# 23 modulation units summed on VectorE beside the feed-forwards, instead of matmuls on TensorE

## The reference, cut to what matters

```python
c_act = silu(c)                                          # one vector of 1024
for i in range(2):
    mod = (c_act @ mod_w[i] + mod_b[i])                  # mod_w[i]: 1024 x 9216
    shift, scale, gate = mod.reshape(1, 3, 3, 1024)[...] # one of each for each of three sublayers
    h = rms_norm(x, g[i,0]) * (1 + scale[0]) + shift[0]
    x = x + 0.5 * gate[0] * ffn(h, i, 0)                 # (silu(h @ w_gate) * (h @ w_up)) @ w_down
    h = rms_norm(x, g[i,1]) * (1 + scale[1]) + shift[1]
    x = x + gate[1] * mixer(h)                           # attention: "fox" for i=0, "dilated" for i=1
    h = rms_norm(x, g[i,2]) * (1 + scale[2]) + shift[2]
    x = x + 0.5 * gate[2] * ffn(h, i, 1)
# then the second block: two layers without modulation
```

## Time and profile before

| | |
|---|---|
| runs of before | 2365.1, 2369.22, 2369.62 us; median 2369.22 |
| profiled execution, its own time | 2364.49 us |
| its span | 2363.2 us |
| TensorE busy (matmuls) | 2260.6 us, 96% |
| VectorE busy | 1327.0 us, 56% |
| ScalarE busy | 1155.3 us, 49% |
| mean DMA rate | 186 GB/s, 439.75 MB |
| mean granted TensorE clock | 0.991 |

### The profile page before, as it was taken

One profiled execution on the slowest core, in us unless ns is written; L12 is line 12 of the kernel. 1 busy time (PEld: TensorE's weight loads), 2 busy tenths in 40 slices (PEclk: granted clock), 3 DMA queues, 4 the chain that ended last, 5 costly groups with the idle time before them and its releaser, 6 DMA issues.

```text
span 2363.2 us, 38278 instructions
## 1 busy us (share of the span) xinstructions
PE 2260.6 (96%) x16752; PEld 2060.3 (87%) x16752; DVE 1327.0 (56%) x1763; ACT 1155.3 (49%) x1348; POOL 57.2 (2%) x72
## 2 busy tenths in 40 slices
PE   6999998999999999899899999999999999999998
PEld 3999866999999987677699997899999988989998
DVE  2543565544455466657555445556786555667873
ACT  3443565543444354544554335654555456436553
POOL 2000000000000000000000011000000020000000
PEclk9999999999999999999999999999999999999999
DMA  8767562666575756345165555433655363445550
GB/s 311 236 229 289 196 250 68 218 223 231 187 252 196 266 192 247 128 150 205 56 214 183 192 196 175 161 125 125 211 182 191 126 233 132 154 143 179 179 196 19
DMA packets 273590, 439.75 MB, mean 186 GB/s; under 512 B 10656, under 2 KB 147152, under 8 KB 273296
## 3 DMA queue, kind: packets, MB, share of 16 engines
q1 hardware_dynamic: 270880, 429.07, 52.6%
q0 software_dynamic: 2256, 7.12, 0.9%
q10 hardware_dynamic: 288, 1.11, 0.1%
HBM read 436.22 MB, written 1.05 MB: 185 GB/s over the span
## 4 chain that ended last, share of the span: by engine, by line
PE 89%; ACT 5%; DVE 3%; DMA 1%; issue 1%; SPq 0%; POOL 0%; ACTq 0%; POOLq 0%; DVEq 0%
PE ps L1265 86%; ACT whi L1487 1%; DVE wlo L1674 1%; PE ps L1418 1%; ACT PT L1487 1%; PE ps L1365 1%; PE ps L1453 1%; DMA raw<-in_mod_w 1%; ACT xhi L1487 1%; PE ps L1428 1%; ACT L1487 1%; ACT S L1487 0%; DMA raw<-in_fox_w_in 0%; SPq L1254 0%; ACT x L1487 0%
## 5 line engine op out<-in xcount | busy, mean ns | idle before, releaser
L1674 DVE TENSOR_TENSOR wlo<-raw,whi 128x2048 fp32r<-128x2048 f32 x339 | 769.0, 2275 | 584.8 <-ACT whi L1487 584.6
L1487 ACT ACTIVATE whi<-raw 128x2048 fp32r<-128x2048 f32 x339 | 640.7, 1895 | 422.4 <-PE ps L1265 387.1
L1265 PE MATMUL ps<-xhi,whi 128*128 128x256 f32 x2888 | 733.5, 286 | 14.8 <-ACT xhi L1487 11.4
L1265 PE MATMUL ps<-xhi,wlo 128*128 128x256 f32 x2888 | 727.9, 284 | 0.0
L1265 PEld LDWEIGHTS ps<-xhi,whi 128*128 128x128 f32 x2888 | 555.7, 192 | 29.1 <-issue 27.6
L1265 PEld LDWEIGHTS ps<-xhi,wlo 128*128 128x128 f32 x2888 | 555.8, 192 | 0.3
L1265 PE MATMUL ps<-xlo,whi 128*128 128x256 f32 x2888 | 471.0, 284 | 3.6 <-DVE xlo L1892 3.4
L1265 PEld LDWEIGHTS ps<-xlo,whi 128*128 128x128 f32 x2888 | 401.4, 192 | 4.3 <-DVE xlo L1892 3.8
L1265 PE MATMUL ps<-hhi,whi 128*128 128x256 f32 x1056 | 299.0, 283 | 0.9 <-DVE modc L1687 0.9
L1265 PE MATMUL ps<-hlo,whi 128*128 128x256 f32 x1056 | 298.5, 283 | 0.0
L1265 PE MATMUL ps<-hhi,wlo 128*128 128x256 f32 x1056 | 297.5, 282 | 0.0
(11 more groups left out here) (222 smaller groups left out, 1999.6 us busy)
## 6 DMA issues: line engine op xcount, KB each, us to landing
raw<-in_mod_w SPq DMA_DIRECT2D x72, 1024.0 KB, 9.2
raw<-in_w_in SPq DMA_DIRECT2D x52, 1024.0 KB, 4.9
raw<-in_ffn_w_gate SPq DMA_DIRECT2D x88, 512.0 KB, 6.5
raw<-in_ffn_w_up SPq DMA_DIRECT2D x88, 512.0 KB, 7.8
raw<-in_ffn_w_down SPq DMA_DIRECT2D x44, 1024.0 KB, 6.7
raw<-in_w_up SPq DMA_DIRECT2D x88, 512.0 KB, 4.7
raw<-in_dil_w_in SPq DMA_DIRECT2D x36, 1024.0 KB, 5.9
raw<-in_w_down SPq DMA_DIRECT2D x22, 1024.0 KB, 4.8
```

Of the source, the lines that this page charges most:

```text
L1265: return nc.tensor.matmul(o, lhs, rhs, start=start, stop=stop, skip_group_check=True)
L1487: return nc.scalar.activation(o, i, func, **kw)
L1674: V.tensor_tensor(wlo[:, s["c"], 0:s["n"]], raw[:, s["slot"], 0:s["n"]], whi[:, s["c"], 0:s["n"]].bitcast(F32), ALU.subtract).then_inc(sem ...
```

## The change

Of the 36 units, 13 stay as they were: the four at the start, the five at norms, and the four within the first mixer. The other 23 are done by VectorE. Each of their two pieces is a step of its own, a `mod_half`: four instructions over 128 x 512 that multiply 512 columns of `raw` by one element of the silu'd `c` per partition and add them to `mrow`. When both halves are in, four matmuls on TensorE with `mrow` as the stationary operand and one column of ones as the moving one sum over the partitions (`mod_sum`), and VectorE adds the bias. A half is planned behind every gateup unit and behind the down pieces 0, 2, 4, ... while there are any: 14 halves in each of the ffn (0,0), (0,1) and (1,0), two in (1,1), and two in the second mixer. `mod_sum` comes when three more projection steps have passed (MOD_LAG), or at the first half of the next unit, whichever is first, or where its result is needed.

```diff
+    def mod_beside(self, i, u, h):
+
+        if h == 0:
+            self.flush_mods()
+        pc = self.take()
+        toks = [self.ev("dve", "mod_acc") for _ in range(4)]
+        self.add("mod_acc", h=h, slot=pc["slot"], landed=pc["landed"], acc_free=self.mod_row_free, acc=toks)
+        self.used(pc, toks[-1])
+        if h:
+            self.mod_turns.append([i, u, 0, lambda: self.mod_sum(i, u, toks[-1])])
+
+    def flush_mods(self):
+        while self.mod_turns:
+            self.mod_turns.pop(0)[3]()
+
+    def mod_sum(self, i, u, acc):
+        bank = self.mod_bank
+        bank_free = self.free[bank]
+        summed = self.mod_row_free = self.ev("pe", "mod_turned")
+        s = self.add("mod_sum", i=i, u=u, bank=bank, bank_free=bank_free, mod_acc=acc, mod_turned=summed,
+                     shift_read=self.shift_read.get(u // 2))
+        self.mod_columns(s, i, u)
+        self.free[bank] = s["mod_bias"]
...
         def ffn(i, j):
...
+            rest = [(*m, h) for m in fill[("ffn", i, j)] for h in range(2)]
+            step("norm", i=i, s=2 * j, m=at_norm.get(("ffn", i, j)))
             for q in range(11):
                 step("gateup", i=i, j=j, q=q)
-                for m in at[q]:
-                    step("mod", i=m[0], u=m[1])
+                half(rest)
             for q in range(11):
                 step("down", i=i, j=j, q=q)
-                if q < 5:
-                    for m in at[11 + q]:
-                        step("mod", i=m[0], u=m[1], bank=G3)
+                if q % 2 == 0:
+                    half(rest)
...
+        elif k == "mod_half":
+            h, u = s["h"], 512 * u
+            self.piece("m", [((4, 512), 0, 512, self.view(a["mod_w"][i], 4 * h, 4 * h + 4, u, u + 512))])
...
+                elif k == "mod_sum":
+                    q.wait_ge(s["mod_acc"])
+                    q.wait_ge(s["bank_free"])
+                    q.wait_ge(("const_set", 5))
+                    for m in range(4):
+                        ins = mm(ps[:, s["bank"], m:m + 1], mrow[:, m * P:(m + 1) * P], epst[:, 2:3], m == 0, True)
                     ins.then_inc(sem["mod_turned"])
...
+                elif k == "mod_acc":
+                    q.wait_ge(("c_silu", 1))
+                    q.wait_ge(s["acc_free"])
+                    q.wait_ge(s["landed"])
+                    v = raw[:, s["slot"], :].rearrange("p (k n) -> p k n", k=4)
+                    for kk in range(4):
+                        c = csil[:, 4 * s["h"] + kk, 0:1]
+                        if s["h"] == 0 and kk == 0:
+                            V.tensor_scalar(mrow[:, :], v[:, kk, :], c, None, ALU.mult).then_inc(sem["mod_acc"])
+                        else:
+                            V.scalar_tensor_tensor(out=mrow[:, :], in0=v[:, kk, :], scalar=c, in1=mrow[:, :], op0=ALU.mult,
+                                                   op1=ALU.add).then_inc(sem["mod_acc"])
+                        q.wait_ge(s["acc"][kk])
```

More of the change, by code:

```diff
@@ L22 @@
 PIECE = 2048
+MOD_LAG = 2
 BIG = 1e30
@@ L29 @@
     "c_in", "mod_in", "ident_in", "x_in", "small_in", "late_in", "out_st",
-    "const_set", "c_silu", "w_hi", "w_lo", "piece", "mod_mm", "mod_row", "mod_turned", "mod_col",
+    "const_set", "c_silu", "w_hi", "w_lo", "piece", "mod_mm", "mod_row", "mod_turned", "mod_col", "mod_acc",
     "square", "stat", "diag", "sqrt", "recip", "rows", "scaled", "x_hi", "x_mod", "x_lo", "resid",
@@ L61, in __init__ @@
         self.mod_row_free = None
+        self.mod_bank = D2
         self.mod_ready = {}
@@ L149, in used, with run_turns, run_mods @@
         self.use += 1
-    def run_turns(self, mod_only=False):
-        while self.turns and not mod_only:
+    def run_turns(self):
+        while self.turns:
             self.turns.pop(0)()
-        while self.mod_turns:
-            self.mod_turns.pop(0)()
+        self.run_mods()
+    def run_mods(self, upto=None):
+        for m in self.mod_turns:
+            m[2] += 1
+        while self.mod_turns and (self.mod_turns[0][2] > MOD_LAG or upto and self.mod_turns[0][:2] <= list(upto)):
+            self.mod_turns.pop(0)[3]()
     def run_beside(self):
@@ L218, in mod_unit @@
             self.used(pc, tok)
-        self.run_turns(True)
+        self.flush_mods()
         row = self.ev("act", "mod_row")
@@ L222, in mod_unit @@
         self.free[bank] = row
-        self.mod_turns.append(lambda: self.mod_turn(i, u, bank, row))
+        self.mod_turns.append([i, u, MOD_LAG, lambda: self.mod_turn(i, u, bank, row)])
     def mod_turn(self, i, u, bank, row):
@@ L232, in mod_turn, with mod_columns @@
         self.free[bank] = col
+        self.mod_columns(s, i, u)
+    def mod_columns(self, s, i, u):
         tok = s["mod_bias"] = self.ev("dve", "mod_col")
@@ L272, in norm @@
         self.pair = 0
+        self.run_mods((i, 6 * s + 3))
         am, bm = self.mod_ready[(i, s, 0)], self.mod_ready[(i, s, 1)]
@@ L328, in down @@
         bank_free = []
+        self.mod_bank = G3
         if q == 0:
@@ L872, in step, with half @@
             steps.append(dict(kind=kind, **kw))
[L874 to L877, removed]
-        def ffn(i, j):
[L880 to L884, removed]
+        fill = {("ffn", 0, 0): [(0, u) for u in range(4, 11)], ("ffn", 0, 1): [(0, 17)] + [(1, u) for u in range(6)],
+                ("ffn", 1, 0): [(1, u) for u in range(7, 14)], ("mix", 1): [(1, 15)], ("ffn", 1, 1): [(1, 17)]}
+        at_norm = {("ffn", 0, 1): (0, 16), ("ffn", 1, 0): (1, 6), ("ffn", 1, 1): (1, 16), ("mix", 0): (0, 11),
+                   ("mix", 1): (1, 14)}
+        def half(rest):
+            if rest:
+                i, u, h = rest.pop(0)
+                step("mod_half", i=i, u=u, h=h)
+        def ffn(i, j):
+            rest = [(*m, h) for m in fill[("ffn", i, j)] for h in range(2)]
+            step("norm", i=i, s=2 * j, m=at_norm.get(("ffn", i, j)))
             for q in range(11):
                 step("gateup", i=i, j=j, q=q)
-                for m in at[q]:
-                    step("mod", i=m[0], u=m[1])
+                half(rest)
             for q in range(11):
                 step("down", i=i, j=j, q=q)
-                if q < 5:
-                    for m in at[11 + q]:
-                        step("mod", i=m[0], u=m[1], bank=G3)
+                if q % 2 == 0:
+                    half(rest)
         def mix(i):
-            fl = list(fill[("mix", i)])
-            step("norm", i=i, s=1, m=fl.pop(0))
+            step("norm", i=i, s=1, m=at_norm[("mix", i)])
             if i == 0:
+                fl = [(0, u) for u in range(12, 16)]
                 for hh in range(2):
@@ L908, in mix @@
             else:
+                rest = [(*m, h) for m in fill[("mix", i)] for h in range(2)]
                 for hh in range(2):
@@ L912, in mix @@
                             step("dil_in", hh=hh, g=g, r=r)
-                        if fl:
-                            m = fl.pop(0)
-                            step("mod", i=m[0], u=m[1])
+                        half(rest)
                     step("dil_attn", hh=hh)
@@ L1013, in lay_out @@
                     tail.flush(0)
-                self.mod_unit(i, u, s.get("bank", D3) - u % 2, CONV if self.in_stage else 0)
+                self.mod_unit(i, u, D3 - u % 2, CONV if self.in_stage else 0)
+            elif k == "mod_half":
+                self.mod_beside(i, u, s["h"])
             elif k == "norm":
@@ L1035, in lay_out @@
                 if s["q"] == FB // 2 - 1:
+                    self.run_mods((i, 12 * s["j"] + 5))
                     tail = Tail(self, self.update("gate", i, 2 * s["j"]), "split" if (i, s["j"]) == (1, 1) else "square")
@@ L1048, in lay_out @@
             elif k == "mix_out":
+                self.mod_bank = G3
                 if u == 1:
+                    self.run_mods((i, 11))
                     tail = Tail(self, self.update("gate", i, 1), "square")
@@ L1365, in pe_program @@
                         ins = nc.tensor.transpose(ps[:, s["bank"], m * P:(m + 1) * P], mrow[:, m * P:(m + 1) * P], ident[:, :])
+                    ins.then_inc(sem["mod_turned"])
+                elif k == "mod_sum":
[4 more added lines that the diff above has]
+                        ins = mm(ps[:, s["bank"], m:m + 1], mrow[:, m * P:(m + 1) * P], epst[:, 2:3], m == 0, True)
                     ins.then_inc(sem["mod_turned"])
@@ L1669, in dve_program @@
             V.memset(epst[:, 1:2], 1e-5).then_inc(sem["const_set"])
+            V.memset(epst[:, 2:3], 1.0).then_inc(sem["const_set"])
             for s in plan.steps:
@@ L1680, in dve_program @@
                     q.wait_ge(s["dve"])
-                elif k == "mod_turn":
+                elif k == "mod_acc":
[11 more added lines that the diff above has]
+                        q.wait_ge(s["acc"][kk])
+                elif k in ("mod_turn", "mod_sum"):
                     i, u, sub, kind = s["i"], s["u"], s["u"] // 6, (s["u"] % 6) // 2
@@ L1686, in dve_program @@
```

(8 more changed lines are left out.)

## The result

After takes 2474.43 us (median of 4, 2470.77 to 2478.22), before 2369.42 in the same session (2365.1 to 2371.05): ratio 1.0454 [1.0437, 1.0471], 4.5% slower. The forecast was 2433; its own range ended at 2465 and its range for 8 in 10 at 2475, so the result lies outside the first and at the very edge of the second. The medians differ by 105 us and the profiled spans by 109.0; the prediction had +67.

The account below looks back on a forecast made before the run. TensorE's matmuls were taken as the bound. Lateness of 122.6 us from a slot loop, less 56.6 removed, plus 1 for sums, gave +67 on 2364.5; adjusted for run offset and noise, 2433 us, 8-in-10 range 2390 to 2475.

Parts of the forecast that it names:

- bursts in the foretold order: Gateup phases: SyncE issues modulation, gate, up, gate, up together, bursts 14.9 us apart.
- The rival without a loop: Whole kernel: slots come free in time and TensorE stays without gaps; 2322 us, chance 0.09.
- VectorE as the bound: VectorE's queue: halves of over 3.4 us set the pace; 2473 us with halves of 4 us, chance 0.06.
- A clock that stays down over most of the ffn: TensorE in the ffn: units take up to 23 us at the low clock; 2600 us, chance 0.03.
- The rival with a shorter loop: Gateup phases: faster halves or sooner landings, turns of 12 to 13.5 us; 2340 to 2390 us, chance 0.08.
- the landing, 7.9: Gateup loop: from slot release until the next modulation and gate pieces, 2 MB, have landed; 7.9 us with SyncE's wake-up.
- Sum 14.9 against T = 11.5: Gateup loop: landing 7.9, conversion 4.2 and half 2.8 make a 14.9 us turn, 3.4 over a gateup unit.
- the 2.6 from W_1's conversion to W_2's: Change to down pieces: the third down piece is converted 2.6 us behind the second, within a 14.4 us interval.
- the prediction's own formula: Each long ffn: lateness is about 11 times the turn's excess over 11.5 us, plus 3.5 us.
- removal less sums: TensorE without the loop: 56.6 us of modulation work removed, about 9 us of sums added; gain 47 us.
- The 0.4: TensorE: price in us of one unit's four one-column sum matmuls, taken from four transposes at 0.44 us.
- 4.0 from the silu to the last conversion's start: VectorE behind a gateup unit: 4.0 us, the first term of a serial path totalling 11.2 us.

Follow-up runs that it names:

- the first experiment: Kernel after, with the half planned ahead of the conversions and only its transfer ensured: 2351.29 us, ratio 0.9941 to before.
- other-bank run: Kernel after, order unchanged, with the sum at gateup 10 in bank G1 instead of D2: 2471.63 us, ratio 1.0448 to before.
- the half first, other bank: Kernel after, with the half planned ahead of the conversions and the sum at gateup 10 in bank G1: 2330.48 us, ratio 0.9846 to before.
- half first, other bank and later sum: Kernel after, with halves ahead of conversions, bank G1 at gateup 10, and two mrow buffers so sums come a unit later: 2344.52 us, ratio 0.9904 to before.

## Why the prediction was wrong in its size

The mechanism held at each step that could be looked at: bursts in the foretold order, `whi` waiting for gate and up transfers in each turn (some 4.6 us for A and 1.0 for B), SyncE on VectorE's half, TensorE idle behind `mrow` (4.3 us in the mean of 15 waits, 6.9 at the longest, where 6 were foretold), second mixer shorter, (1,1) within 1 us of before. The rival without a loop (2322) fell by the result and by turns of 15.7, VectorE as the bound by the first experiment and the stretch above. A clock that stays down over most of the ffn is not what the trace shows: its mean is 0.90 in the first ffn (60 to 275 us, 1.00 before) and 0.962 over the whole. The rival with a shorter loop had the sign of the error wrong. What failed are two terms that were put too low: the landing, 7.9, in the step "Sum 14.9 against T = 11.5", and the 2.6 from W_1's conversion to W_2's at the change to down pieces.

- **The turn: 15.7, not 14.9** (means of eight turns: 15.68 in ffn (0,0), 15.49 in (0,1), 15.87 in (1,0)). The conversion was right: `whi` 97.83, `wlo` 99.77 to 102.06, 4.23. The half was taken as 2.8; it adds 2.8 (first half) and 3.05 (second) to the turn, 2.9 in the mean, since a pass with the scalar of each partition takes 0.75 and not the 0.69 of the nearest row. The landing was taken as 7.9 and is 8.5 in the mean of the first ffn, 0.6 of the 0.8: 89.59 to 97.83 is 8.2, as in most turns, and two had 9.5 and 9.3. In those two 2.86 and 2.69 MB had moved by the landing, in the others 2.38 to 2.46, of which A and the half's piece are 2.10; why more moved in them is open. By the prediction's own formula 0.8 more a turn is 3 x 11 x 0.8 = 26 us: +93 in place of +67.
- **The change to down pieces.** Predicted intervals between the ends of the halves M_9 to M_12: 14.4, 11.9, 14.5. Measured: 17.4, 12.3, 16.0 (214.79, 232.22, 244.55, 260.57). The first is 3.0 short because the working there forgot that gateup 10 has an epilogue. ScalarE in order:

```profile
219.74 1.91 ACT L1538 ACTIVATE whi<-raw 128x2048 fp32r<-128x2048 f32 x1 [10.32 <-DMA raw<-in_ffn_w_down]
221.56 0.58 ACT L1538 ACTIVATE e<-ps 128x512 f32<-128x512 f32 x1
224.68 0.63 ACT L1538 ACTIVATE hhi<-e 128x512 fp32r<-128x512 f32 x1 [2.54 <-DVE e L1825]
225.21 1.89 ACT L1538 ACTIVATE whi<-raw 128x2048 fp32r<-128x2048 f32 x1
```

  The conversion of W_2 doesn't follow that of W_1: silu, product and copy stand between them, and they wait on each other across the two queues, 5.5 us from one `whi` to the next. The prediction's 2.6 is 5.5. Of the 5.0 us too little over three intervals some 2.4 are the longer turn, counted above; 2.6 are new, some 8 us for three ffn. Sum +101 of the 109. The run without the half at gateup 10 says the place was worth 7 us an ffn.
- **W_0 and its clock.** TensorE stood 9.47 us before W_0, for the bias step of bank D2. The prediction saw the sum's wait for the half, not the bank's way back through VectorE's queue:

```profile
214.82 1.86 PE L1309 MATMUL ps<-epst,mrow 128*128 128x1 f32 x8 [3.99 <-DVE mrow L1743]
226.16 0.58 PE L1309 MATMUL ps<-hhi,whi 128*128 128x256 f32 x1 [9.47 <-DVE modc L1759]
```

```profile
215.00:230.00 15.00, 5.53 (x26) 5.44 (x27) 6.48 (x7) 4.83 (x4) 0.00 (x0) 0.50 0.56 210
```

  The granted clock is 0.50, 1.2 GHz, over that stretch. The other-bank run shows that this wait added nothing while the loop ran. The remaining 8 us of the 109 I can't place. With each ffn's own turn, 2.2, 2.1 and 2.6 us stay in the three ffn and the rest outside them; starts at the low clock are a candidate, and no run separates them. The Trainium skill ("TensorE: Matmul & The Clock Gate", section "HAM oscillation — how this bites in real kernels") has bursts with DMA waits between them starting cold each time; the rows here agree for the long gaps (0.50 behind 9.47 us) and not for every unit, since from 60 to 90 us the clock stays at 1.00 with TensorE idle for 4.0 of the 30 us.
- **The removal and the sum.** Out of the loop (the half first, other bank) the gain is 1.54%, 36 us, where removal less sums was put at 47. The price of the sums accounts for it: eight records in 0.95 us, 0.8 from the first to the work behind it (86.24 to 87.05 in that run), and not 0.4. 23 x 0.8 = 18, and 56.6 - 18.4 = 38, within 2 of the 36 measured. The 0.4 came from a row that isn't the same kind of work: four transposes are four records there, four of these matmuls are eight, each with a weight load of 128 x 128. At the low clock the eight take 1.86.
- **The landing by the skill.** The Trainium skill, "DMA: Bandwidth & Descriptors", section "Anatomy of one DMA", has about 2 us and bytes over 436 GB/s, and gives that fit for transfers issued by GpSimd; these are SyncE's. An estimate by it for the 2 MB is 6.8. The trace of after has 8.2 and more. With 0.79 MB less the estimate is 1.8 us less; the run has 1.1. It is too short for a piece inside these bursts, and the measurement decides.
- **A slip that changes nothing.** The prediction's "4.0 from the silu to the last conversion's start" is 3.8 by the earlier trace rows; its 11.2 is the sum with 3.8.

## What to carry to other kernels

Before work is moved to an idle engine, ask what that engine's place in the queue does to the buffers: a slot of an in-order ring that is freed behind a step which itself needs a later transfer closes a loop, and the loop's turn, not the share of any engine, is then the pace. Such a loop is found on paper by asking of each release "what must have landed before it?", and it is opened by order: here three lines let the user of the slot go first (121 us), where another bank or a second buffer brought nothing that the intervals show and shorter terms of the loop (half the passes, a quarter of the transfer) gave some 55 us each. Inside this loop the two edits that didn't touch its turn were worth nothing; outside it one of them paid (0 and 22 us for the bank), so the loop is to be opened first and the rest priced again.

## What the runs showed of the hardware that wasn't expected

- The half's scalar_tensor_tensor over 128 x 512, with a scalar for each partition, takes 751 ns; the product of two tensors of this shape takes 685. What in it costs the 66 ns wasn't tested.
- Four fp32 matmuls with one moving column cost about 0.8 us at full clock and 1.86 at 1.2 GHz. They are eight records, so 0.10 us each, hardly less than the 0.12 from one float32r matmul of 256 columns to the next.
- In a burst of 3 MB the 2 MB that are wanted first land after 8.2 us, sometimes 9.5, and 2.4 to 2.9 MB have moved by then. The burst shown above ends with 2 us in which the DMA share is 0.08 and 0.05.
- Behind a gap of 5.03 us in TensorE's work (ahead of the sum at 120.33) the matmuls came 0.21 us apart, at 0.41 each, up to 124.97; at full clock it is 0.12 and 0.28. Behind the gap of 9.47 us this lasted from 226.16 to 230.79. In the run with half first, other bank and later sum the wait of 2.87 us stands in a stretch (180 to 195 us) with a mean granted clock of 0.89.
